# Seven block products instead of eight for the values of a gated mixer, in groups two to four

## The reference, cut to what matters

```python
h = rms_norm(x, a_norm) * (1.0 + scale) + shift        # 2048 x 1024
u, v, z = jnp.split(h @ w_in, 3, axis=-1)              # w_in: 1024 x 6144, v: 2048 x 2048
u = jax.nn.gelu(u)
v = layer_norm(jax.nn.gelu(v), ln_g, ln_b)
mixed = jnp.einsum("gts,bnsgc->bntgc", ws, vc) + b_s.T[:, :, None]   # vc: v in chunks of 128 tokens
y = u * mixed.reshape(B, S, A_WIDTH) * jax.nn.silu(z)
x = x + gate * (y @ w_out)                             # w_out: 2048 x 1024
```

## Time and profile before

| | |
|---|---|
| median of 3 runs | 2301.33 us (2300.05 to 2304.97) |
| the profiled execution's own time | 2302.98 us |
| its span, first to last instruction | 2301.3 us |
| TensorE busy | 2233.4 us, 97% |
| DVE, ACT, POOL busy | 56%, 39%, 40% |
| clock granted to TensorE, mean | 0.996 of full speed |
| bytes moved | 460.68 MB, 200 GB/s over the span |

### The profile page before, as it was taken

One profiled execution on the slowest core, in us unless ns is written; L12 is line 12 of the kernel. 1 busy time (PEld: TensorE's weight loads), 2 busy tenths in 40 slices (PEclk: granted clock), 3 DMA queues, 4 the chain that ended last, 5 costly groups with the idle time before them and its releaser, 6 DMA issues.

```text
span 2301.3 us, 28399 instructions
## 1 busy us (share of the span) xinstructions
PE 2233.4 (97%) x10726; PEld 1875.8 (82%) x10726; DVE 1293.7 (56%) x1772; ACT 887.7 (39%) x1694; POOL 911.7 (40%) x576
## 2 busy tenths in 40 slices
PE   5999999999999999999999999998999999999998
PEld 4888878888888888888888888786888888887886
DVE  5757752415864413786241686435666657656754
ACT  4323342433343433434253334323444434444442
POOL 2445454444554354545445445330222232232222
PEclk9999999999999999999999999999999999999999
DMA  8743442543465353456344355759586797776654
GB/s 332 271 169 128 150 170 83 176 147 125 170 216 177 105 188 124 156 194 223 114 138 144 117 181 204 264 195 335 214 324 214 273 340 257 249 300 253 219 202 164
DMA packets 205159, 460.68 MB, mean 200 GB/s; under 512 B 17152, under 2 KB 93024, under 8 KB 204640
## 3 DMA queue, kind: packets, MB, share of 16 engines
q1 hardware_dynamic: 202064, 453.58, 55.6%
q10 hardware_dynamic: 2960, 5.30, 0.6%
HBM read 359.19 MB, written 90.18 MB: 195 GB/s over the span
## 4 chain that ended last, share of the span: by engine, by line
PE 89%; DVE 4%; DMA 3%; issue 1%; ACT 1%; DVEq 1%; POOLq 0%; SPq 0%; POOL 0%; ACTq 0%
PE ps L1553 26%; PE ps L1555 26%; PE ps L1554 26%; PE ps L1718 3%; DMA w_raw<-in_a_w_out 1%; PE ps L1756 1%; PE ps L1757 1%; PE ps L1782 1%; DVE acc L1176 1%; DMA r<-kv_input 1%; DVE y_hl L1348 1%; PE ps L1791 1%; PE ps L1792 1%; PE ps L1794 1%; PE ps L1793 1%
## 5 line engine op out<-in xcount | busy, mean ns | idle before, releaser
L743 POOL TENSOR_TENSOR w_lo<-w_raw,w_hi 128x1024 fp32r<-128x1024 f32 x256 | 647.6, 2540 | 772.3 <-ACT w_hi L867 772.0
L867 ACT ACTIVATE w_hi<-w_raw 128x1024 fp32r<-128x1024 f32 x256 | 271.6, 1061 | 700.5 <-DMA w_raw<-in_a_w_in 457.4
L1553 PE MATMUL ps<-h,w_hi 128*128 128x512 f32 x1024 | 401.6, 392 | 0.0
L1555 PE MATMUL ps<-h,w_lo 128*128 128x512 f32 x1024 | 398.8, 389 | 0.0
L1554 PE MATMUL ps<-h,w_hi 128*128 128x512 f32 x1024 | 398.5, 389 | 0.0
L816 POOL TENSOR_SCALAR_AFFINE_SELECT pt<-pt 128x512 fp32r<-128x512 f32 x128 | 82.9, 648 | 394.4 <-ACT pt L1107 341.8
L1555 PEld LDWEIGHTS ps<-h,w_lo 128*128 128x128 f32 x1024 | 192.2, 188 | 40.5
L1554 PEld LDWEIGHTS ps<-h,w_hi 128*128 128x128 f32 x1024 | 192.3, 188 | 39.5 <-issue 0.2
L1553 PEld LDWEIGHTS ps<-h,w_hi 128*128 128x128 f32 x1024 | 192.3, 188 | 39.1 <-issue 0.2
L1553 PE MATMUL ps<-w_hi,h 128*128 128x512 f32 x512 | 201.6, 394 | 5.3 <-DVE h L1204 5.3
L1553 PE MATMUL ps<-w_hi,y_hl 128*128 128x512 f32 x512 | 201.8, 394 | 2.5 <-POOL w_lo L743 2.5
(11 more groups left out here) (214 smaller groups left out, 4102.1 us busy)
## 6 DMA issues: line engine op xcount, KB each, us to landing
w_raw<-in_a_w_in SPq DMA_DIRECT2D x256, 256.0 KB, 3.1
w_hi<-b_weights_split SPq DMA_DIRECT2D x104, 512.0 KB, 4.2
w_lo<-b_weights_split SPq DMA_DIRECT2D x104, 512.0 KB, 5.9
w_raw<-in_a_w_in SPq DMA_DIRECT2D x64, 512.0 KB, 4.7
w_raw<-in_a_w_out SPq DMA_DIRECT2D x64, 512.0 KB, 4.1
kv_input<-xks SPq DMA_DIRECT2D x32, 512.0 KB, 6.6
b_input<-hbs SPq DMA_DIRECT2D x32, 512.0 KB, 7.5
r<-b_input SPq DMA_DIRECT2D x16, 1024.0 KB, 11.3
```

Of the source, the lines that this page charges most:

```text
L743: g.tensor_tensor(wlo[p][:, rows_], raw[p][:, rows_], whi[p][:, rows_].bitcast(F32), ALU.subtract).then_inc(w_lo, 1)
L867: s_.activation(whi[p][:, rows_], raw[p][:, rows_], ACT.Copy).then_inc(w_hi, 1)
L1553: t_.matmul(dst_, stat[0], mov[0], start=start, stop=False)
L1555: return t_.matmul(dst_, stat[1], mov[0], start=False, stop=stop)
```

## The change

In groups two to four, each half of the columns of `v` (1024 columns) is computed as a two by two block product with seven products (the Winograd form) and not eight. The blocks are 256 tokens by 512 by 512. A product is one unit of 4 pieces, 24 matmuls; a group has 14 of them for its `v`. Group one stays as it was.

With `h11, h12, h21, h22` the blocks of `h` (tokens, columns) and `B11 ..` those of the weights, the products of a half are, in order of `m`: 0 `h11*B11`, 1 `h12*B21`, 2 `s2*T`, 3 `h22*T`, 4 `s1*T`, 5 `s4*B22`, 6 `s3*T`, where `s1..s4` are sums of blocks of `h` and the four `T` are sums of blocks of weights.

- **Weights.** The `T` are formed in group one (`comb`, 8 steps: DVE forms, ACT and POOL split, SP keeps them in DRAM as `cbd`) and then loaded as two parts of 1 MB each per product, straight into `w_hi` and `w_lo`. Products 0, 1 and 5 of each half go the old way through `hi` and `lo`.
- **Sums of `h`.** DVE forms `s1..s4` (`s_add`, one drain ahead of every step), ACT rounds them (`s_round`), DVE makes their rests (`s_rest`).
- **Outputs.** ACT copies product 0's banks to SBUF (`ut`); DVE adds the others to it one after another (`block_out`, 14 additions of 128x512 per half), in `ut`, `ue` and `vy`; ACT applies GELU to `vy` in place.
- **Moved.** The next `x` is loaded at the end of the `uz` stage, squared after `y_round(3)` and scaled after `y_rest(3)`; in groups two to four the tables are made in the `v` stage; the two splits of stages 1 and 2 go to 4 and 5; the stores of `x1` come after the load of unit 3; the last `a_residual` comes after `s_rest(i, 0)`.

The core of the diff (removed lines with `-`):

```diff
+V_UNITS = [8] + [14] * (NG - 1)
+FACTORS = [("B", 0, 0), ("B", 1, 0), ("T", 3), ("T", 2), ("T", 0), ("B", 1, 1), ("T", 1)]
+def pieces_in(u):
+    return 4 if product_of(u) is not None else 8
@@ SP
+                if kept_split(u):
+                    sv, m = product_of(u)
+                    for part, w in ((0, whi[p]), (1, wlo[p])):
+                        sp.dma_start(w[:, 2 * hh:2 * hh + 2].bitcast(F32), cbd[sv, FACTORS[m][1], hh, part]) \
+                            .then_inc(raw_in[2 * p + hh], 16)
...
+                    for n in range(2, V_UNITS[i]):
+                        unit(v_unit(i, n))
+                        if n == 3:
+                            for cnk in range(NC):
+                                sp.wait_ge(ao_read, at("ao_read", i - 1, cnk + 5))
+                                sp.dma_start(x1d[i - 1, :, cnk], x1[:, cnk, :]).then_inc(x1_out, 16)
@@ POOL
+                    x1_stage(i - 1)
+                    for n in range(2, V_UNITS[i]):
+                        if not kept_split(v_unit(i, n)):
+                            lo(v_unit(i, n))
@@ ACT
+                def v_blocks(sv):
+                    for c in range(2):
+                        act.wait_ge(piece_done, pieces(v_unit(i, 7 * sv), 3 + c))
+                        if sv:
+                            act.wait_ge(block_sum, sums(i, 0, 13))
+                        s_.activation(ut[:, c, :], bank(2 * sv + c), ACT.Copy).then_inc(first_kept, 1)
+                    if sv == 0:
+                        s_round(i, 1)
+                        x1_squares(i - 1)
+                    for c in range(2):
+                        gelu(sv, c, 2 * sv, 1 + c)
+                    if sv == 0:
+                        s_round(i, 2)
+                        s_round(i, 3)
+                    hi(v_unit(i, 7 * sv + 5))
+                    for c in range(2):
+                        gelu(sv, c, 2 * sv + 1, 9 + c)
+                    after = (v_unit(i, 7), v_unit(i, 8)) if sv == 0 else (uz_unit(i, 0, 0), uz_unit(i, 0, 1))
+                    hi(after[0])
+                    for c in range(2):
+                        gelu(sv, 2 + c, 2 * sv + 1, 11 + 2 * c)
+                        gelu(sv, 2 + c, 2 * sv, 12 + 2 * c)
+                        hi(after[1], (c,))
+                if i >= 1:
+                    s_round(i, 0)
+                    v_blocks(0)
+                    v_blocks(1)
@@ DVE
+            def s_add(s, q, terms):
+                there = S_SUMS[s][:, 2 * q:2 * q + 2, 1, :]
+                before = terms[0][1]
+                for op, term in terms[1:]:
+                    dve.drain()
+                    last = v.tensor_tensor(there, before, term, op)
+                    before = there
+                last.then_inc(s_sum, 1)
+                def v_blocks(sv):
+                    j = 2 * sv
+                    block_out(sv, 1, lambda c: v_chunk(j, c), flat(ut))
+                    if sv == 0:
+                        s_fourth(0)
+                        s_fourth(1)
+                    else:
+                        table(i, 0)
+                    block_out(sv, 2, flat(ut), flat(ut))
+                    if sv == 0:
+                        s_rest(i, 2)
+                        s_third(0)
+                        s_third(1)
+                    block_out(sv, 3, flat(ue), flat(ut))
+                    if sv == 0:
+                        s_rest(i, 3)
+                    else:
+                        table(i, 1)
+                    for c in range(2):
+                        v_stat(j, c, 8 * sv + c + 1)
+                    block_out(sv, 4, flat(ut), flat(ut))
+                    if sv == 0:
+                        x1_scale(i - 1)
+                    block_out(sv, 5, lambda c: v_chunk(j + 1, c), flat(ut))
...
                 else:
-                    v_stats(0)
-                    x1_scale(i - 1)
-                    for j in range(1, 4):
-                        v_stats(j)
+                    s_rest(i, 0)
+                    a_residual(i - 1, 1, 3)
+                    s_rest(i, 1)
+                    v_blocks(0)
+                    last_stats(0)
+                    v_blocks(1)
+                    last_stats(1)
...
-                for cnk in range(NC):
+                for cnk in range(NC - 1):
                     if i < NG - 1:
                         h_rest(i + 1, 2 * cnk)
                         h_rest(i + 1, 2 * cnk + 1)
-                    a_residual(1, cnk)
+                    a_residual(i, 1, cnk)
+                if i < NG - 1:
+                    s_first(0)
+                    h_rest(i + 1, 6)
+                    s_second(0)
+                    h_rest(i + 1, 7)
+                    s_first(1)
+                    s_second(1)
```

More of the change, by code:

```diff
@@ L36, with group_of, v_unit, uz_unit @@
 PI_BELOW = 3.1415925
-U_V, U_UZ, U_AO, A_UNITS = 0, 8, 24, 32
-FIRST_B = A_UNITS * NG
+V_UNITS = [8] + [14] * (NG - 1)
+FIRST = [sum(V_UNITS[:i]) + 24 * i for i in range(NG + 1)]
+FIRST_B = FIRST[NG]
+PRODUCTS = 7
+FACTORS = [("B", 0, 0), ("B", 1, 0), ("T", 3), ("T", 2), ("T", 0), ("B", 1, 1), ("T", 1)]
+def group_of(u):
+    return max(i for i in range(NG) if FIRST[i] <= u)
+def v_unit(i, n):
+    return FIRST[i] + n
+def uz_unit(i, g, ku):
+    return FIRST[i] + V_UNITS[i] + 2 * g + ku
+def ao_unit(i, k, n):
+    return FIRST[i] + V_UNITS[i] + 16 + 2 * k + n
+def product_of(u):
+    if u >= FIRST_B:
+        return None
+    i = group_of(u)
+    n = u - FIRST[i]
+    return (n // PRODUCTS, n % PRODUCTS) if i >= 1 and n < V_UNITS[i] else None
+def kept_split(u):
+    product = product_of(u)
+    return product is not None and FACTORS[product[1]][0] == "T"
 def b_order():
@@ L120, with comb_at, comb_before @@
 SPLITS = 2 * len(SPLIT_UNITS)
-SPLIT_STAGES = [(i, q) for i in range(NG) for q in ((1, 2) if i else ()) + (6, 7, 8, 9, 10)]
+SPLIT_STAGES = [(i, q) for i in range(NG) for q in range(4 if i else 6, 11)]
 FIRST_GATED = 2 * SPLIT_UNITS.index(("b", 0, 0))
+COMB_STAGES = [2, 4, 5, 6, 7, 8, 9, 10]
+COMB_PLACE = [q % 2 for q in COMB_STAGES]
+def comb_at(i, q):
+    return COMB_STAGES.index(q) if i == 0 and q in COMB_STAGES else None
+def comb_before(c):
+    return COMB_PLACE[:c].count(COMB_PLACE[c])
 def split_at(i, q):
@@ L193 @@
 SMALL = 1408
+QT = T // 2
 def step_of(a):
@@ L464, in keep_y, with transfers @@
             eng.dma_start(out[0, T * g + P * cnk:T * g + P * cnk + P, :], xr_of(g, cnk)).then_inc(y_out, 16)
+        def transfers(u):
+            if u >= FIRST_B or kept_split(u):
+                return 2
+            i = group_of(u)
+            return 2 if uz_unit(i, 0, 0) <= u < ao_unit(i, 0, 0) else 1
         def landed(u):
-            return 16 * sum(2 if w >= FIRST_B or U_UZ <= w % A_UNITS < U_AO else 1 for w in range(u % 2, u + 1, 2))
+            return 16 * sum(transfers(w) for w in range(u % 2, u + 1, 2))
         @block.sync
@@ L753, in split, with comb @@
                 g.tensor_tensor(wsl[m][:], wsr[m][:], wsh[m][:].bitcast(F32), ALU.subtract).then_inc(split_lo, 1)
+            def comb(i, q):
+                c = comb_at(i, q)
+                if c is None:
+                    return
+                m = COMB_PLACE[c]
+                pool.wait_ge(comb_hi, c + 1)
+                for half in range(2):
+                    rows_ = slice(2 * half, 2 * half + 2)
+                    last = g.tensor_tensor(cbl[m][:, rows_], cbr[m][:, rows_], cbh[m][:, rows_].bitcast(F32), ALU.subtract)
+                last.then_inc(comb_lo, 1)
             def rstd(dst_, src, tmp, signal):
@@ new lines, in s_rest, with s_whole @@
+            def s_rest(i, s):
+                for q in range(2):
+                    there = S_ORDER[s][:, 2 * q:2 * q + 2]
+                    dve.drain()
+                    dve.wait_ge(s_hi, s_parts(i, s, q))
+                    v.tensor_tensor(there[:, :, 1, :], S_SUMS[s][:, 2 * q:2 * q + 2, 1, :],
+                                    there[:, :, 0, :].bitcast(F32), ALU.subtract).then_inc(s_lo, 1)
+            def s_whole(s, q, part):
+                return S_ORDER[s][:, 2 * q:2 * q + 2, part, :].bitcast(F32)
@@ L1621, in unit @@
             def unit(u, piece, bank_free=None, after=None):
-                for k in range(8):
+                for k in range(pieces_in(u)):
                     j, hh = order(u, k)
-                    if k in ((0, 4) if by_halves(u) else (0, 1)):
-                        pe.wait_ge(w_lo, 2 * u + hh + 1)
+                    if k in starts(u):
+                        if kept_split(u):
+                            pe.wait_ge(raw_in[2 * (u % 2) + hh], landed(u))
+                        else:
+                            pe.wait_ge(w_lo, 2 * SPLIT_HERE[u] + hh + 1)
                     if hh == 0 and bank_free is not None:
```

411 lines of the change are left out of this document (288 added, 123 removed).

## The result

The changed kernel takes 2333.33 us, the median of four runs (2329.88 to 2336.03), beside 2300.69 for the kernel before (2299.78 to 2304.97): ratio 1.0137, 95% interval 1.0117 to 1.0158. The forecast was 2314 with a range up to 2331. The direction was right, the size short by more than half: 33 us were lost, 13 foretold.

What follows compares the result with a forecast made beforehand. TensorE, busy 97%, was taken to bound the kernel. Stages of 38.4 + 49.0 + 3.6 = 91.0 us against 87.2 add 11.4 in three groups; with the median offset and uncounted handovers, 2314 us, 8-in-10 range 2287 to 2331.

Steps and rivals of the forecast that it cites:

- The removed work: Value stages of groups two to four: 336 matmuls for 384, 5.45 us a product, saving 10.9 us a group.
- The other edits, at nothing: Group one's `comb` steps and the moved loads, splits and tables cost nothing; bounds -2 us and +5.
- Product 1: Start of the value stage: weights wanted at 5.45, half of them ready at 7.9, so 2.5 us lost whatever DVE does.
- DVE's chain: Start of each value stage: 36 operations, 27.7 us, ending at t = 34.0 with POOL's delays.
- product 5: Value stage: starts at 38.4, without waits 27.2; waits of products 1, 2 and 4 lie inside these 11.2 us.
- The named cause: On ACT, `hi` of product 5's weights stands behind `s_round(3)`, which needs the last `s_third`; product 5 starts at 38.4.
- the gap ahead of product 5: Sign in the value stages: a TensorE gap there that ends with `w_lo`, with ACT idle until `s_round(3)`.
- The DMA rival: Value stages: stores of `x1` and 385 GB/s of loads meet; 3 to 4 us a group more, 2325; chance 0.18.
- Later waits: Value stage from product 5 on: waits at products 5, 7, 12, 13 and the first `uz` unit, together 3.6 us.

Runs made afterwards that it cites:

- the filled one: Changed kernel plus throwaway matmuls ahead of products 1 and 4 in the value stages of groups two to four: ratio 1.0103 to the kernel before.

## Why the prediction fell short

*The removed work* was right: 5.45 us a product without waits.

*Group one is the step that failed*, "The other edits, at nothing", with bounds of -2 and +5; it cost +15.9. I listed POOL's 5 us a step and asked only whether POOL and DVE had the time. In the value stage I did reckon that a POOL subtraction holds DVE up; I didn't apply the same row here, where eight steps each add two such operations right behind others. That TensorE waits in the mixer stage for `vs` alone was the warning, not the cover: `vs` comes from DVE.

*Product 1* was to wait 2.5 at least, for weights; it waited 5.0 for `h`, held by POOL. With `h` first it waited 1.8 to 2.5: the floor was about right, the forecast of what stands on it wasn't. Nor did it lie inside product 5's delay at no cost: without it product 5 starts 2.4 to 3.6 us earlier.

*DVE's chain* ended at t = 33.0 against 34.0, *product 5* started at 40.6, 41.3 and 40.1 against 38.4. The named cause, `hi` behind `s_round(3)`, was not what held it: its weights landed 3.3 us after ACT was free. That cause is the second bound (37.7 with the stores late). Nor was there the gap ahead of product 5 by which the forecast was to be known: TensorE idled 0.2 to 0.3 us there, and lost its time at products 1 and 4. The DMA rival was right on the place: the stores of `x1` push product 4's load and all behind it. I had counted 2.2 us of it as hidden; it is 3.2 to 4.1 plus the clock, and is not.

*Later waits*: stage less product 5's start less nine products of 5.45 leaves 3.4, 2.0 and 2.0 us, 3.6 forecast. Close enough.

*Not seen at all*: the granted clock. The half-speed steps cost 2.5 to 3.0 us in product 1 and 1.6 to 2.1 in product 4 of each group. By the experiment they decide only 0.8 to 2.1 us of a stage here, as DVE, ACT and DMA would otherwise have been late.

The value stages thus came to +15.1 against +12.6. That they came so near is in part luck: the end of DVE's chain was right, but it was not what held product 5, and the delays that did hold it happened to add up to nearly as much. Of the miss of 20 us, 15.9 are group one, 2.5 these stages and 2 the rest.

## What to carry to other kernels

Ask of work added to GpSimd not whether GpSimd has room but which VectorE operations run beside it, and who waits for these: here 47 us of subtractions at 46% load cost 19.7 us of TensorE. Where TensorE's stage is shortened by an eighth, look for several bounds stacked within a few us (here landing, ScalarE's order, VectorE's chain); mending one gives only the distance to the next. And a wait of a few us on TensorE costs more than its length, by the slow matmuls behind it; but count that as gain only where the other engines could keep up, which here they did for 0.8 to 2.1 us of 4 to 5.

## What the runs showed of the hardware that was not expected

TensorE drops to 1.2 GHz (steps of 0.427 us) after short waits in a stage that is otherwise dense. Over the value stages of 13 profiled executions (all but the filled one), of 27 waits of 1.0 to 1.95 us (the step from the matmul before, less 0.227) one was followed by a slow step; of 38 of 2.1 to 4.0 us, 34 were, and lost 1.9 us on average beside the wait; of 33 of 4.0 to 5.2 us all were, 2.4 us on average, 3.0 at most. The Trainium skill, "TensorE: Matmul & The Clock Gate", What's actually happening, says that an idle engine falls to half rate, which agrees.

A `TENSOR_SCALAR` of DVE on 512 f32 columns, with one tensor input, took 2.46 us beside POOL (the row at 201.79) where one alone takes 0.43. The earlier trace rows had shown such an operation held up at 1024 columns; the price is a POOL operation's length, so the short ones are stretched most.
